# Row one-hots of eight tokens as one VectorE comparison, and the low parts of 64 table blocks on GpSimd

## The chip, the cores and the metric

The kernel runs on one core of a Trainium2 chip. The metric is the device time of one execution in microseconds (us). Three runs of the kernel before took 2293.08, 2294.5 and 2297.16 us; their median, 2294.5 us, is the time to compare with.

## The reference, cut to what matters

The reference is one layer of a hybrid network over 128 prompt tokens and 512 sample tokens of width 1024. Its last part is a mixer of 16384 experts, and the change touches only that part:

```python
q = (x @ wq).reshape(T, 8, 2, 128)                    # 8 heads, two half queries
s = einsum('thpd,hpkd->thpk', q, sub_keys)            # scores against 2 x 128 keys
s_top, i_top = top_k(s, 16)                           # pairs of keys -> best 16 experts
idx  = i_top[..., 0, a] * 128 + i_top[..., 1, b]      # expert = 128 * i + j
gate = softmax(best)
a = gelu(einsum('td,tkd->tk', x, u_tab[idx]))         # 128 chosen experts a token
y = einsum('tk,tkd->td', gate * a, v_tab[idx])
```

## The kernel before, in words

For the 512 sample tokens the kernel does not gather rows. It multiplies the whole table `u` with the tokens: 128 blocks of 128 experts, `ps = u_block x h2` (K = 1024 in 8 steps `k` of 128, N = 512 tokens), takes the gelu and stores the result (`a_dram`). To keep the accuracy of float32, each operand is split in a high part (a cast to fp32r) and a low part (the rest), and each step `k` has three matmuls: `uhi*h2hi`, `uhi*h2lo`, `ulo*h2hi` (L906). A block of `u` is loaded by SP (`load_u`, L516, 512 KB), ScalarE casts it (`uhi`, L1682), and another engine subtracts (`ulo = uraw - uhi`). In blocks 0 to 40 that engine is GpSimd (L1812), from block 41 on it is VectorE (L1417). `uhi` and `ulo` have two buffers each, `uraw` four.

In blocks 40 to 103, the gate stage, the dense gate matrix of each of the 512 sample tokens is built besides, eight tokens a block. For one token the 128 chosen experts stand on the partitions with their numbers i and j and their gate. `eA[:, q]` (128x128) has the gate where the column equals i, else 0, and `eB[:, k]` has 1 where the column equals j: each is a comparison of `iota` with one column of `cols_hk`. The matmul `eB x eA` (L946) gives the 128x128 gates of the token. It stands behind step `k` of the block's products (`gate_matrix(k)`), so that in each block eight steps of three products and one gate matrix follow each other on TensorE. `eA` is a ring of 8 matrices, `eB` two groups of eight. Four tokens fill a PSUM bank; ScalarE copies it to `gst` (L1708), and when eight blocks are done SP stores the half in two DMAs of 2 MB (`store_g`, L543), the first behind the block whose number is 7 modulo 8, the second behind the next. Before each of them SP has stored the block's gelu output (`store_a`, L521) and loaded block n+4.

Who makes what in the gate stage before the change:

- VectorE, per block (`step_b`): eight `eA` (L1452), the two `eB` with q % 4 == 3 (L1451), behind the fifth token `split_u` of block n+1 (L1417), and two `dot` (L1426). A dot is a product-sum of 1024 elements of one gathered row for each of the 128 prompt tokens, `ugat` with `h2row`. Its loop over four groups of 16 blocks is one body run without a loop and then a hardware loop of three passes; a pass begins with copies of the group's columns to `jcur` and `cur`, since an address that depends on the loop counter is only used there.
- GpSimd, per block: the other six `eB` (L1855), and two `gather_u` (L1824), indirect DMAs of 128 rows of 4 KB, 512 KB each, into a ring of four slots. The gathers behind the six `eB` of block m (counted from the first gate block) are those for the dots of block m+1. A gather waits until the dot that used its slot is done.
- ScalarE, per block: `split_u(n+1)` (`uhi`), two copies to `gst`, and the gelu (L1692), in this order.
- SP, per block: `store_a(n)`, `load_u(n+4)`, and where due `store_g`.

TensorE waits at the start of a block for `uhi` and `ulo` of the block, and before a gate matrix for its `eA` and `eB`. VectorE may write `eA` of token q when the gate matrix of token q-8 is done. The order on each engine is the order of the program; nothing reorders it.

Of the kernel before, what the change touches and what calls it, by code (L numbers as in the profile page):

```python
# [8 lines left out]
ALU = mybir.AluOpType  # L9
# [8 lines left out]
P = 128  # L18
# [54 lines left out]
POOL_ROWS = TB - TB // 4  # L73

CAND = [(0, 2, 16), (2, 2, 8), (4, 4, 4), (8, 8, 2)]
NCAND = sum(na * nb for _, na, nb in CAND)


def dve_row(q):
    return q % 4 == 3  # L80
# [14 lines left out]
def bass_hybrid_layer(nc, x, cvec, w_ada, w_in, w_out, w_q, cols, hfcols, hf_w1, hf_w2, hf_w3,  # L95
# [7 lines left out]
    with ctx:  # L103
# [71 lines left out]
        cur = at("cur", 134, [P, 3, 128])  # L175
        jcur = at("jcur", 136, [P, 128])
# [222 lines left out]
        cur_ready = sem("cur_ready")  # L399
# [21 lines left out]
        jcur_ready = sem("jcur_ready")  # L421
# [185 lines left out]
        def _(pe):  # L607
# [324 lines left out]
            def step_b(it, first):  # L932
                for b in range(NB_B):

                    def gate_matrix(k):
# [7 lines left out]
                        if not dve_row(q):  # L943
                            pe.wait_ge(onehot_j_ready, (it * NB_B + b) * POOL_ROWS + k - k // 4 + 1)
# [47 lines left out]
        def _(dve):  # L992
# [426 lines left out]
            def dot(it, k, first):  # L1419

                if k == 0 and not first:
                    dve.wait_ge(dots_gelu, it)
                if not (first and k == 0):
                    dve.wait_ge(dot_done, it * DOTS_IT + k)
                dve.wait_ge(u_gathered[k % GSLOT], it * (16 * DOTS_IT // GSLOT) + 16 * (k // GSLOT + 1))
                dve.tensor_tensor_reduce(junk[:], ugat[:, k % GSLOT], h2row[:], 1.0, 0.0, ALU.mult, ALU.add,  # L1426
                                         dots[:, k:k + 1]).then_inc(dot_done, 1)

            def slot_weights(it):

                hk = bass.ds(it * DOTS_IT, DOTS_IT)
                dve.wait_ge(dots_gelu, it + 1)
                dve.tensor_tensor(w0[:, hk], acur[:], gate0[:, hk], ALU.mult).then_inc(w0_ready, 1)

            def step_b(it, first):
                if not first:
                    dve.wait_ge(onehot_j_ready, it * POOL_ROWS * NB_B)
                    dve.wait_ge(onehot_ready, it * P)
                dd = bass.ds(it * P, P)
                dve.tensor_copy(jcur[:], cols_hk[:, 1, dd]).then_inc(jcur_ready, 1)  # L1440
                dve.tensor_copy(cur[:], cols_hk[:, :, dd]).then_inc(cur_ready, 1)
                dve.wait_ge(cur_ready, it + 1)
                for b in range(NB_B):
                    n = it * NB_B + b + BLK_A
                    for k in range(TB):
                        q = TB * b + k
                        tok = it * P + q
                        if not (first and q < RING):
                            dve.wait_ge(onehot_used, tok + 1 - RING)
# [6 lines left out]
                    if b == 2 and not first:  # L1456
                        slot_weights(it - 1)
                    for e in range(DOTS_B):
                        dot(it, DOTS_B * b + e, first)

            loop(dve, NTD, step_b)
# [321 lines left out]
        def _(pool):  # L1783
# [161 lines left out]
```

## Time and profile before

| | |
|---|---|
| median of three runs | 2294.5 us |
| the profiled execution: its own time / span | 2292.26 / 2290.5 us |
| TensorE matmul busy, share of the span | 2173.6 us, 95% |
| VectorE busy | 1438.7 us, 63% |
| ScalarE busy | 623.6 us, 27% |
| GpSimd busy | 796.5 us, 35% |
| mean granted TensorE clock | 0.976 |
| moved by DMA | 475.54 MB, 208 GB/s over the span |

Matmuls overlap, so a busy TensorE is not one at its peak. The gate stage lasts from 917.8 to 1442 us of the span. The stages behind it are the other 24 blocks of `u` and the second products with the table `v`.

### The profile page before, as it was taken

The page shows a single profiled execution, that of the slowest core. Times are in us where ns is not written, and L with a number is a line of the kernel's source. Part 1 is how long each engine was busy: PE and PEld are TensorE (multiplying, and loading weights), DVE is VectorE, ACT ScalarE, POOL GpSimd, SP SyncE. Part 2 cuts the span into 40 slices and gives each one's busy share as a digit, 9 for nine tenths or more (in the row PEclk, how much of TensorE's full clock was granted, in tenths as well). Part 3 has the DMA queues.
Part 4 walks back from the last instruction along what each step waited for, and adds up shares of the span by engine and source line. Part 5 has one row for each costly group of instructions (what it writes and reads, how often), then busy time and mean ns, then how long its engine had stood idle before and what let it go on. Part 6 is the DMA issues. An engine that isn't in the chain of part 4 may idle for free.

```text
span 2290.5 us, 30680 instructions
## 1 busy us (share of the span) xinstructions
PE 2173.6 (95%) x9868; PEld 1665.6 (73%) x9868; DVE 1438.7 (63%) x3055; ACT 623.6 (27%) x930; POOL 796.5 (35%) x713
## 2 busy tenths in 40 slices
PE   7999998798989999999999898999999999999998
PEld 3554444546987877877777787787888888888886
DVE  4221426334889998878777787324766666666665
ACT  2111012333222223333333233223323222222222
POOL 0000001003225554998989898001222212121220
PEclk7999999898999999999999999999999999999999
DMA  9122124204204444699997899855988888888883
GB/s 338 45 74 72 44 85 181 97 33 160 75 1 153 144 139 138 205 301 309 297 282 250 270 298 288 254 174 210 352 285 294 285 291 289 289 288 290 288 289 146
DMA packets 293477, 475.54 MB, mean 208 GB/s; under 512 B 148871, under 2 KB 150055, under 8 KB 292872
## 3 DMA queue, kind: packets, MB, share of 16 engines
q1 hardware_dynamic: 256520, 340.20, 45.1%
q0 software_dynamic: 36864, 134.23, 16.6%
q8 instruction: 42, 0.69, 0.1%
q14 instruction: 51, 0.42, 0.1%
HBM read 401.76 MB, written 72.61 MB: 207 GB/s over the span
## 4 chain that ended last, share of the span: by engine, by line
PE 78%; POOL 9%; DVE 5%; DMA 3%; issue 2%; SPq 2%; ACT 1%; DVEq 0%; ACTq 0%; POOLq 0%
PE ps L965 30%; PE ps L906 19%; POOL eB L1855 6%; PE ps L624 5%; PE ps L717 3%; PE ps L843 3%; POOL ugat L1824 3%; PE ps L878 3%; PE ps L879 3%; PE ps L683 2%; PE ps L946 2%; SPq L521 2%; PE ps L623 1%; DMA uraw<-in_u_t 1%; PE ps L666 1%
## 5 line engine op out<-in xcount | busy, mean ns | idle before, releaser
L906 PE MATMUL ps<-h2hi,uhi 128*128 128x512 f32 x1024 | 449.8, 439 | 20.3 <-DVE scores L1375 7.7
L906 PE MATMUL ps<-h2hi,ulo 128*128 128x512 f32 x1024 | 404.9, 395 | 0.0
L965 PE MATMUL ps<-vhi,whi 128*128 128x512 f32 x1024 | 399.2, 390 | 5.6 <-DVE wlo L1475 5.6
L906 PE MATMUL ps<-h2lo,uhi 128*128 128x512 f32 x1024 | 403.7, 394 | 0.0
L965 PE MATMUL ps<-vhi,wlo 128*128 128x512 f32 x1024 | 399.1, 390 | 0.0
L965 PE MATMUL ps<-vlo,whi 128*128 128x512 f32 x1024 | 399.0, 390 | 0.0
L1832 POOL DMA_INDIRECT vgat<-in_v_tab,idx x128 | 145.4, 1136 | 660.0 <-DVE y L1485 508.3
L1855 POOL TENSOR_SCALAR eB<-iota,jcur 128x128 f32<-128x128 f32 x384 | 318.1, 841 | 18.8 <-DVE jcur L1440 17.0
L1473 DVE TENSOR_TENSOR vlo<-vraw,vhi 128x1024 fp32r<-128x1024 f32 x128 | 156.8, 1225 | 216.6 <-ACT vhi L1748 216.6
L1748 ACT ACTIVATE vhi<-vraw 128x1024 fp32r<-128x1024 f32 x128 | 135.5, 1061 | 465.8 <-PE ps L965 464.0
L946 PEld LDWEIGHTS ps<-eA,eB 128*128 128x128 f32 x1024 | 192.2, 191 | 93.0 <-POOL eB L1855 25.6
L946 PE MATMUL ps<-eA,eB 128*128 128x128 f32 x1024 | 202.4, 279 | 35.4 <-DVE eA L1452 24.6
L906 PEld LDWEIGHTS ps<-h2hi,uhi 128*128 128x128 f32 x1024 | 196.8, 192 | 44.5 <-issue 21.1
L965 PEld LDWEIGHTS ps<-vhi,whi 128*128 128x128 f32 x1024 | 192.6, 188 | 46.8 <-issue 6.8
L906 PEld LDWEIGHTS ps<-h2hi,ulo 128*128 128x128 f32 x1024 | 194.7, 190 | 43.0
L1417 DVE TENSOR_TENSOR ulo<-uraw,uhi 128x1024 fp32r<-128x1024 f32 x87 | 109.5, 1258 | 182.9 <-ACT uhi L1682 180.5
L965 PEld LDWEIGHTS ps<-vlo,whi 128*128 128x128 f32 x1024 | 192.6, 188 | 40.1
L965 PEld LDWEIGHTS ps<-vhi,wlo 128*128 128x128 f32 x1024 | 192.5, 188 | 40.1
L906 PEld LDWEIGHTS ps<-h2lo,uhi 128*128 128x128 f32 x1024 | 197.0, 192 | 19.9
L1426 DVE CUSTOM_DVE_ANT_0 junk<-ugat,h2row 128x1024 f32<-128x1024 f32 x128 | 157.5, 1230 | 24.6 <-DMA ugat<-in_u_rows,idx 21.8
L1452 DVE TENSOR_SCALAR eA<-iota,cur 128x128 f32<-128x128 f32 x512 | 168.2, 372 | 0.4
L1708 ACT ACTIVATE gst<-ps 128x512 f32<-128x512 f32 x128 | 76.5, 598 | 329.5 <-PE ps L946 329.5
(270 smaller groups left out, 2993.7 us busy)
## 6 DMA issues: line engine op xcount, KB each, us to landing
uraw<-in_u_t SPq DMA_DIRECT2D x128, 512.0 KB
vraw<-in_v_tab SPq DMA_DIRECT2D x128, 512.0 KB
gelu_scratch<-aout SPq DMA_DIRECT2D x128, 256.0 KB
gate_scratch<-gst SPq DMA_DIRECT2D x16, 2048.0 KB, 14.9
ain<-gelu_scratch SPq DMA_DIRECT2D x128, 256.0 KB, 4.1
gin<-gate_scratch SPq DMA_DIRECT2D x128, 256.0 KB, 4.4
wring<-in_w_ada SPq DMA_DIRECT2D x12, 2048.0 KB, 10.6
wring<-in_w_in SPq DMA_DIRECT2D x6, 2048.0 KB, 8.5
```

The source lines that it names most:

```text
L624: s_ = pe.matmul(bank(us)[0:m], w, as_, start=(j == 0), stop=(j == n - 1))
L906: last = pe.matmul(ps[:, b % 4, :], w[:, b % 2, k, :], h[:, k, LP:T], start=(k == 0 and j == 0), stop=(k == KD - 1 and j == 2))
L946: pe.matmul(o_, eB[:, b % 2, k], eA[:, q % RING], start=True, stop=True).then_inc(onehot_used, 1)
L965: last = pe.matmul(ps[:, y_bank(t) + h, :], w[:, b, (t - 1) * P:t * P], v[:, b, h * 512:(h + 1) * 512], start=(start and j == 0), stop=(st ...
L1417: dve.tensor_tensor(ulo[:, b % 2], uraw[:, b % 4], uhi[:, b % 2].bitcast(F32), ALU.subtract).then_inc(ulo_ready, 1)
L1426: dve.tensor_tensor_reduce(junk[:], ugat[:, k % GSLOT], h2row[:], 1.0, 0.0, ALU.mult, ALU.add, dots[:, k:k + 1]).then_inc(dot_done, 1)
L1452: dve.tensor_scalar(eA[:, q % RING], iota[:], cur[:, 0, q:q + 1], cur[:, 2, q:q + 1], ALU.is_equal, ALU.mult).then_inc(onehot_ready, 1)
L1473: dve.tensor_tensor(vlo[:, s], vraw[:, s], vhi[:, s].bitcast(F32), ALU.subtract).then_inc(vlo_ready, 1)
L1708: act.activation(gst[:, half, :, off:off + 4], ps[:, 4 + quad % 4, :].rearrange("p (q i) -> p i q", q=4), ACT.Copy).then_inc(gate_staged, 1)
L1748: act.activation(vhi[:, s], vraw[:, s], ACT.Copy).then_inc(vhi_ready, 1)
L1832: pool.indirect_dma_start(out=vgat[:, k % GSLOT], out_offset=None, in_=v_tab, in_offset=bass.IndirectOffsetOnAxis(ap=idx0[:, k:k + 1], axis=0)
L1855: pool.tensor_scalar(eB[:, b % 2, k], iota[:], jcur[:, TB * b + k:TB * b + k + 1], None, ALU.is_equal).then_inc(onehot_j_ready, 1)
```

## The change

Three things change, all in the gate stage:

1. `eB` of all eight tokens of a block is one VectorE instruction (`slot_keys`), a `tensor_tensor` comparison of 128x1024 elements whose two inputs are broadcast views of `iota` and of eight columns of `cols_hk`. It is written one block ahead. GpSimd writes no `eB`. TensorE waits for it once a block.
2. The low parts `ulo` of blocks 41 to 104 are made by GpSimd, in front of the two gathers of its step; VectorE takes over again from block 105.
3. VectorE's loop over groups is written out (64 blocks one after another), without `cur` and `jcur`; the columns are read from `cols_hk`.

```diff
-                        if not dve_row(q):
-                            pe.wait_ge(onehot_j_ready, (it * NB_B + b) * POOL_ROWS + k - k // 4 + 1)
+                        if k == 0:
+                            pe.wait_ge(onehot_j_ready, it * NB_B + b + 1)
...
-            def step_b(it, first):
-                if not first:
-                    dve.wait_ge(onehot_j_ready, it * POOL_ROWS * NB_B)
-                    dve.wait_ge(onehot_ready, it * P)
-                dd = bass.ds(it * P, P)
-                dve.tensor_copy(jcur[:], cols_hk[:, 1, dd]).then_inc(jcur_ready, 1)
-                dve.tensor_copy(cur[:], cols_hk[:, :, dd]).then_inc(cur_ready, 1)
-                dve.wait_ge(cur_ready, it + 1)
-                for b in range(NB_B):
...
-                        if dve_row(q):
-                            dve.tensor_scalar(eB[:, b % 2, k], iota[:], cur[:, 1, q:q + 1], None, ALU.is_equal)
-                        dve.tensor_scalar(eA[:, q % RING], iota[:], cur[:, 0, q:q + 1], cur[:, 2, q:q + 1],
-                                          ALU.is_equal, ALU.mult).then_inc(onehot_ready, 1)
-                        if k == 4:
-                            split_u(n + 1, b + 1)
...
-            loop(dve, NTD, step_b)
+            def slot_keys(m):
+                if m >= 2:
+                    dve.wait_ge(onehot_used, TB * (m - 1))
+                dve.tensor_tensor(eB[:, m % 2], iota[:].unsqueeze(1).broadcast_to([P, TB, 128]),
+                                  cols_hk[:, 1, TB * m:TB * (m + 1)].unsqueeze(2).broadcast_to([P, TB, 128]),
+                                  ALU.is_equal).then_inc(onehot_j_ready, 1)
+            slot_keys(0)
+            for n in range(BLK_A, BLK_C):
+                m = n - BLK_A
+                for k in range(TB):
+                    q = TB * m + k
+                    if q >= RING:
+                        dve.wait_ge(onehot_used, q + 1 - RING)
+                    dve.tensor_scalar(eA[:, q % RING], iota[:], cols_hk[:, 0, q:q + 1], cols_hk[:, 2, q:q + 1],
+                                      ALU.is_equal, ALU.mult).then_inc(onehot_ready, 1)
+                if m % NB_B == 2 and m >= NB_B:
+                    slot_weights(m // NB_B - 1)
+                if n + 1 < BLK_C:
+                    slot_keys(m + 1)
+                for e in range(DOTS_B):
+                    dot(DOTS_B * m + e)
+            dve.wait_ge(ulo_ready, BLK_C + 1)
...
             for n in range(NTD * NB_B):
-                it, b = n // NB_B, n % NB_B
-                if b == 0:
-                    pool.wait_ge(jcur_ready, it + 1)
-                if n >= 2:
-                    pool.wait_ge(onehot_used, TB * (n - 1))
-                for k in range(TB):
-                    if not dve_row(TB * b + k):
-                        pool.tensor_scalar(eB[:, b % 2, k], iota[:], jcur[:, TB * b + k:TB * b + k + 1], None, ALU.is_equal
-                                           ).then_inc(onehot_j_ready, 1)
+                split_u(BLK_A + n + 1, n + 1, False)
                 if n:
                     for e in range(DOTS_B):
                         gather_u(DOTS_B * (n - 1) + e + GSLOT)
```

## Rows read from the trace of the kernel before

**Rows 1.** Busy time in a window, the gate stage (columns in the first line).

```profile
core 0: us, PE busy (x) PEld busy (x) DVE busy (x) ACT busy (x) POOL busy (x), PEclk, DMA share, GB/s
917.80:1442.00 524.20, 488.83 (x2571) 408.44 (x2570) 410.61 (x971) 168.26 (x259) 466.64 (x508) 0.98 0.89 277
```

**Rows 2.** Timeline of ScalarE (start, length): gelu of four blocks; 919.92 and 1442.48 are 64 blocks apart.

```profile
919.92 0.60 ACT L1692 ACTIVATE aout<-ps 128x512 f32<-128x512 f32 x1 [8.58 <-PE ps L906]
971.75 0.59 ACT L1692 ACTIVATE aout<-ps 128x512 f32<-128x512 f32 x1
...
979.08 0.59 ACT L1692 ACTIVATE aout<-ps 128x512 f32<-128x512 f32 x1
979.56 1.06 ACT L1682 ACTIVATE uhi<-uraw 128x1024 fp32r<-128x1024 f32 x1
...
1442.48 0.59 ACT L1692 ACTIVATE aout<-ps 128x512 f32<-128x512 f32 x1
```

**Rows 3.** Timeline of GpSimd, one block of a stretch without gate stores.

```profile
1206.86 5.47 POOL L1855 TENSOR_SCALAR eB<-iota,jcur 128x128 f32<-128x128 f32 x6
1212.50 1.91 POOL L1824 DMA_INDIRECT ugat<-in_u_rows,idx  x1 [0.17 <-issue]
1214.71 0.94 POOL L1824 DMA_INDIRECT ugat<-in_u_rows,idx  x1 [0.30 <-issue]
1215.68 5.24 POOL L1855 TENSOR_SCALAR eB<-iota,jcur 128x128 f32<-128x128 f32 x6
```

**Rows 4.** Timeline of VectorE and TensorE, start of VectorE's third and fourth passes.

```profile
1173.02 0.23 DVE L1440 COPY jcur<-cols_hk 128x128 f32 x1 [3.34 <-issue]
1174.32 0.71 PE L946 MATMUL ps<-eA,eB 128*128 128x128 f32 x2 [3.36 <-DVE eA L1452]
1311.83 0.23 DVE L1440 COPY jcur<-cols_hk 128x128 f32 x1 [2.79 <-issue]
```

**Rows 5.** Timeline of SP's queue, around the first pair of gate stores, and the last.

```profile
980.64 2.11 SPq L543 DMA_DIRECT2D gate_scratch<-gst  x1
987.03 6.35 SPq L521 DMA_DIRECT2D gelu_scratch<-aout  x1
993.90 0.49 SPq L543 DMA_DIRECT2D gate_scratch<-gst  x1
994.44 13.03 SPq L521 DMA_DIRECT2D gelu_scratch<-aout  x1
1242.93 0.38 SPq L543 DMA_DIRECT2D gate_scratch<-gst  x1
1376.22 0.38 SPq L543 DMA_DIRECT2D gate_scratch<-gst  x1
1444.42 9.01 SPq L543 DMA_DIRECT2D gate_scratch<-gst  x2
```

**Rows 6.** Chain of waits, the three late table blocks (start, length).

```profile
1007.56 7.05 DMA uraw<-in_u_t
1272.35 8.75 DMA uraw<-in_u_t
1403.42 9.27 DMA uraw<-in_u_t
```

**Rows 7.** Timeline of ScalarE, VectorE and TensorE at the first late block.

```profile
1014.64 1.06 ACT L1682 ACTIVATE uhi<-uraw 128x1024 fp32r<-128x1024 f32 x1 [4.64 <-DMA uraw<-in_u_t]
1015.73 1.42 DVE L1417 TENSOR_TENSOR ulo<-uraw,uhi 128x1024 fp32r<-128x1024 f32 x1 [5.30 <-ACT uhi L1682]
1017.51 0.80 PE L946 MATMUL ps<-eA,eB 128*128 128x128 f32 x2 [3.36 <-DVE eA L1452]
1019.39 0.63 PE L946 MATMUL ps<-eA,eB 128*128 128x128 f32 x2
1020.98 0.39 PE L946 MATMUL ps<-eA,eB 128*128 128x128 f32 x2
```

**Rows 8.** Timeline, blocks 0 to 40: GpSimd's subtraction alone, and beside VectorE.

```profile
705.51 2.45 POOL L1812 TENSOR_TENSOR ulo<-uraw,uhi 128x1024 fp32r<-128x1024 f32 x1 [3.05 <-ACT uhi L1682]
710.95 4.47 POOL L1812 TENSOR_TENSOR ulo<-uraw,uhi 128x1024 fp32r<-128x1024 f32 x1 [2.99 <-ACT uhi L1682]
710.88 2.29 DVE L1364 TENSOR_TENSOR oneh<-work,iota 128x2048 f32<-128x2048 f32 x1
713.21 4.35 DVE L1367 TENSOR_TENSOR oneh<-oneh,itopf 128x2048 f32<-128x2048 f32 x1
```

**Rows 9.** Timeline of VectorE: second dots of three blocks that waited for their rows.

```profile
1082.29 1.23 DVE L1426 CUSTOM_DVE_ANT_0 junk<-ugat,h2row 128x1024 f32<-128x1024 f32 x1 [0.65 <-DMA ugat<-in_u_rows,idx]
1138.04 1.23 DVE L1426 CUSTOM_DVE_ANT_0 junk<-ugat,h2row 128x1024 f32<-128x1024 f32 x1 [0.78 <-DMA ugat<-in_u_rows,idx]
1246.66 1.23 DVE L1426 CUSTOM_DVE_ANT_0 junk<-ugat,h2row 128x1024 f32<-128x1024 f32 x1 [0.55 <-DMA ugat<-in_u_rows,idx]
```

**Rows 10.** Timeline of GpSimd: the gathers of those rows, in the same order.

```profile
1073.95 0.94 POOL L1824 DMA_INDIRECT ugat<-in_u_rows,idx  x1 [0.30 <-issue]
1129.25 0.94 POOL L1824 DMA_INDIRECT ugat<-in_u_rows,idx  x1 [0.30 <-issue]
1240.37 0.94 POOL L1824 DMA_INDIRECT ugat<-in_u_rows,idx  x1 [0.30 <-issue]
```

More of the change, by code:

```diff
@@ L174, in bass_hybrid_layer @@
         eB = at("eB", 126, [P, 2, TB, 128])
-        cur = at("cur", 134, [P, 3, 128])
-        jcur = at("jcur", 136, [P, 128])
         gst = at("gst", 139, [P, 2, 128, 64])
@@ L398, in bass_hybrid_layer @@
         dot_done = sem("dot_done")
-        cur_ready = sem("cur_ready")
         dots_gelu = sem("dots_gelu")
@@ L420, in bass_hybrid_layer @@
         onehot_used = sem("onehot_used")
-        jcur_ready = sem("jcur_ready")
         gate_full = sem("gate_full")
@@ L1417, in split_u, with dot @@
                 dve.tensor_tensor(ulo[:, b % 2], uraw[:, b % 4], uhi[:, b % 2].bitcast(F32), ALU.subtract).then_inc(ulo_ready, 1)
[L1419 to L1426, printed above, removed]
+            def dot(g):
+                r, k = g // DOTS_IT, g % DOTS_IT
+                if k == 0 and r:
+                    dve.wait_ge(dots_gelu, r)
+                if g:
+                    dve.wait_ge(dot_done, g)
+                dve.wait_ge(u_gathered[g % GSLOT], 16 * (g // GSLOT + 1))
+                dve.tensor_tensor_reduce(junk[:], ugat[:, g % GSLOT], h2row[:], 1.0, 0.0, ALU.mult, ALU.add,
@@ L1427, in dot, with slot_weights @@
                                          dots[:, k:k + 1]).then_inc(dot_done, 1)
-            def slot_weights(it):
-                hk = bass.ds(it * DOTS_IT, DOTS_IT)
-                dve.wait_ge(dots_gelu, it + 1)
+            def slot_weights(r):
+                hk = slice(r * DOTS_IT, (r + 1) * DOTS_IT)
+                dve.wait_ge(dots_gelu, r + 1)
                 dve.tensor_tensor(w0[:, hk], acur[:], gate0[:, hk], ALU.mult).then_inc(w0_ready, 1)
-            def step_b(it, first):
-                if not first:
-                    dve.wait_ge(onehot_j_ready, it * POOL_ROWS * NB_B)
-                    dve.wait_ge(onehot_ready, it * P)
-                dd = bass.ds(it * P, P)
-                dve.tensor_copy(jcur[:], cols_hk[:, 1, dd]).then_inc(jcur_ready, 1)
-                dve.tensor_copy(cur[:], cols_hk[:, :, dd]).then_inc(cur_ready, 1)
-                dve.wait_ge(cur_ready, it + 1)
-                for b in range(NB_B):
-                    n = it * NB_B + b + BLK_A
-                    for k in range(TB):
[L1446 to L1449, printed above, removed]
-                        if dve_row(q):
-                            dve.tensor_scalar(eB[:, b % 2, k], iota[:], cur[:, 1, q:q + 1], None, ALU.is_equal)
-                        dve.tensor_scalar(eA[:, q % RING], iota[:], cur[:, 0, q:q + 1], cur[:, 2, q:q + 1],
-                                          ALU.is_equal, ALU.mult).then_inc(onehot_ready, 1)
-                        if k == 4:
-                            split_u(n + 1, b + 1)
[L1456 to L1459, printed above, removed]
@@ L1847, in _ @@
             for n in range(NTD * NB_B):
-                it, b = n // NB_B, n % NB_B
-                if b == 0:
-                    pool.wait_ge(jcur_ready, it + 1)
-                if n >= 2:
-                    pool.wait_ge(onehot_used, TB * (n - 1))
-                for k in range(TB):
-                    if not dve_row(TB * b + k):
-                        pool.tensor_scalar(eB[:, b % 2, k], iota[:], jcur[:, TB * b + k:TB * b + k + 1], None, ALU.is_equal
-                                           ).then_inc(onehot_j_ready, 1)
+                split_u(BLK_A + n + 1, n + 1, False)
                 if n:
```

3 lines of the change are left out of this document (removed).

## The prediction

> **What bounds the kernel now.** I read the page first (TensorE is busy nearly all the time, so only a stage in which it idles can change), then the windows of the gate stage, ScalarE's timeline as a clock of the blocks, the waits, and the timelines of each engine where a block was long. In the window of the gate stage TensorE is busy 488.8 of 524.2 us, GpSimd 466.6, and the DMA engines 0.89 of the time at 277 GB/s [rows 1]. So three things are close to full at once, and the question is which of them ends each block.
>
> The starts of ScalarE's gelu tell the pace. An undisturbed block takes 979.08 - 971.75 = 7.33 us, all of it TensorE. The 64 blocks take 1442.48 - 919.92 = 522.6 us against 64 x 7.33 = 469.1 [rows 2]. The excess, 53.5 us, is all that the change can win in this stage, and it has three sources:
> - *GpSimd's own pace.* In a stretch without gate stores one round of six `eB` and two gathers lasts 1215.68 - 1206.86 = 8.8 us [rows 3]. That is 1.5 more than a block of TensorE; between 1204 and 1242 us there are five such blocks, and elsewhere the same work mostly takes less than 7.33: about 8 us in all.
> - *VectorE's loop passes.* At the third and fourth pass VectorE starts nothing for 3.34 and 2.79 us and TensorE's next gate matrix comes 3.36 us late [rows 4]. With the slow clock behind it (below) the two blocks are 4.6 and 5.2 us long: 10 us. TensorE and ScalarE cross their own loop ends there without a gap of their own.
> - *Gate stores.* Behind each 2 MB store SP's next issue is held: 6.35 us, then 13.03 [rows 5]. So the table block five blocks on is asked for 27 us after the first store (1007.56 - 980.64) and lands 7.05 to 9.27 us later [rows 5, 6]. That is the rest, 53.5 - 8 - 10 = 35 us over seven pairs of stores.
>
> **Part 1, the end of GpSimd's `eB` and of the loop.** Six `eB` of about 0.9 us (5.47 / 6) [rows 3] leave GpSimd; the 8 us of slow rounds go. The written-out loop has no pass ends: 10 us go, but both lie in or near a pair of stores, and what the stores cost does not vanish with them. The Trainium skill says on "Runtime: NRT & Kernel Launch" (Instruction fetch mechanics) that a taken branch out of the prefetched window stalls until the page is fetched; rows 4 agree, and by that rule alone the 10 us would be won in full.
>
> **Part 2, one comparison on VectorE.** The same kind of instruction (two broadcast views, `is_equal`) takes 2.29 us for 2048 elements [rows 8], so 1.15 for 1024. VectorE loses `ulo` (about 1.23) and two small `eB`. It has 8 `eA`, 1.15 and two dots of 1.23 in 7.33 us, some 5.8: no bound. It runs nearly a block ahead of TensorE, so this is hidden. What is gained: before, `split_u` stood in the middle of VectorE's row. When a table block was late, VectorE waited in it 5.30 us and the sixth gate matrix of the block *before* the late one came 3.36 us late [rows 7]. After, this block runs to its end.
>
> **Part 3, `ulo` on GpSimd.** Alone it takes 2.45 us [rows 8]; `uhi` starts 0.48 behind the gelu and takes 1.06 [rows 2]. It needs to be there when the next block starts and is, by over 2 us. The subtraction itself is hidden. But two gathers are queued behind it. Count from the first gate matrix of block m, at 0 (the gelu of the block before starts then too). `uhi` of block m+1 ends at 1.54, `ulo` at 4.0, the gathers are issued at 4.15 and, with the spacing of rows 3 when nothing holds the first, 5.5. Their rows are for the dots of block m+1, and behind these dots stand the `eA` of block m+2. From issue to use a gather needs L; then a dot (1.23) and an `eA` (0.35). So the first gate matrix of block m+2, due at 14.67, is free at 5.5 + L + 1.6 = 7.1 + L. TensorE keeps its pace if L is below 7.6. L read from dots that waited: 6.29 us in a stretch without stores (1246.66 - 1240.37), 8.34 and 8.79 beside them (1082.29 - 1073.95, 1138.04 - 1129.25) [rows 9, 10]. Quiet blocks pass; beside stores two blocks cost 7.1 + 8.6 - 14.67 = 1.0 us more, hidden behind the late table block.
>
> **A pair of stores after the change.** Time from the first store, t = 0. The late block lands at 34.0, 38.2 or 36.5 (1007.56 + 7.05 - 980.64, 1272.35 + 8.75 - 1242.93, 1403.42 + 9.27 - 1376.22) [rows 5, 6], mean 36.2. Then `uhi` 1.06, `ulo` 2.45 and the handoffs, 0.4: TensorE starts the block at 40.1. At its own pace it would have been there at 34.4 (five blocks from 979.08, less the 0.7 of the first products, less 980.64). Stall: 5.7 us. After a stall TensorE runs at the lower of its two levels for a while: the gate matrices of rows 7 are 1.88 and 1.59 us apart, against 0.92. That adds 1.7. Third, the gathers for this block's dots were behind the late `ulo`: issued 0.1 and 1.45 behind the start of the block. With L = 8.3 the next block's first gate matrix is free 1.45 + 8.3 + 1.6 = 11.35 behind it; TensorE would want it at 8.0 + 1.7 = 9.7. That adds 1.65. Before, the gathers went out during the stall and were never late behind it. Sum: 5.7 + 1.7 + 1.65 = 9.05 us a pair, 7 pairs in the stage: 63.4 us.
>
> **The sum.** Excess before 53.5, after 63.4: +9.9 us on the profiled execution's 2292.26, so 2302. Its time lies 2.2 us below the median of the runs shown, inside their spread of 4; I leave that. The costs not seen before: L in a block just behind a stall, from 6.3 to 8.8, is -1.65 to +0.5 a pair, -12 to +4; the landing from 34.0 to 38.2 is -2.2 to +2.0 a pair, -15 to +14. VectorE's new wait for `eB`'s buffer is met before it is reached.
>
> **The port.** A subtraction of GpSimd that met a two-input VectorE instruction took 4.47 instead of 2.45, and the VectorE instruction behind it 4.35 instead of 2.29 [rows 8]: each waited for the other's end. In the gate stage the two-input instructions are short (1.15 to 1.23), so `ulo` can come up to 1.2 later. The Trainium skill ("SBUF — State Buffer", on VectorE and GpSimd contention) calls this an exclusive lock held for the whole instruction, taken with two SBUF inputs; by it, `eB` on VectorE would hold GpSimd's subtraction in every block, which is the third rival.
>
> **The rivals.**
> - *The gathers are in time (faster).* If L behind a stall is about 6.3, the third term is 0; and with every landing as the first (34.0) the stall is 3.5. Then 3.5 + 1.7 = 5.2 a pair, 36 in all, 17 less than before: 2275; with the landings half way, 2285. For it: the 6.29 of the quiet stretch, and VectorE no longer coupled to the table's load. Against: three table loads and three gelu stores are issued at once just when the gathers go. It decides at L = 6.7.
> - *The stores set the pace of the half-group.* If TensorE, early or late, meets the same store end, won and lost cancel: 2290 to 2297. For it: the half-groups of before are 66.3 us on average ((1444.42 - 980.64) / 7) [rows 5], with and without a loop end in them.
> - *The port decides.* With `ulo` held 1.2 in every block the bound is 8.3 + L for two blocks; at L = 7.3 that is 0.45 a block more, for the 29 blocks away from stores 13, and 1.2 for each pair: +21 on the forecast, 2323, less where VectorE's dots have moved away: 2315 to 2323. Against it: when the dots come later, they leave the time of `ulo` free.
>
> **How the numbers follow.** A difference under 0.2% (4.6 us) can't be told from none. The forecast, slower (2298 to 2309), has 0.38, the port 0.10, the stores' pace 0.16, the gathers in time 0.36. That gives slower 0.48, same 0.16, faster 0.36. The likeliest is 2302. The range reaches over the gathers' case to 2277 and into the port's to 2318.
>
> **What would show it.** After the change: GpSimd's rounds well under 7.33 us with waits for `uhi` in front of `ulo`; no gap in VectorE at the pass ends; undisturbed blocks at 7.33; at a late table block, TensorE waiting for `ulo` at the start of the block instead of at the sixth gate matrix; behind it dots waiting for their gather and TensorE for `eA`. I am wrong if these dots don't wait (then it is faster), if `ulo` takes over 3 us in most blocks, or if the late table block lands at another time than 34 to 38 us behind the first store.

## The result, and the profile after

The changed kernel took 2318.95 us (median of 8 runs, 2304.12 to 2338.19), the kernel before 2293.79 us in the same session (8 runs). The ratio is 1.0113, with a 95% interval of 1.008 to 1.0145: slower, as forecast, but by 25 us instead of 10, and 1 us outside the range. The profiled execution took 2312.91 us, 20.65 more than that of before.

The starts of the gelu on ScalarE's timeline again give the pace (start, length). 919.86 and 1460.92 are 64 blocks apart, the middle two are neighbours:

```profile
919.86 0.60 ACT L1681 ACTIVATE aout<-ps 128x512 f32<-128x512 f32 x1 [8.56 <-PE ps L896]
...
1166.21 0.59 ACT L1681 ACTIVATE aout<-ps 128x512 f32<-128x512 f32 x1
1174.11 0.59 ACT L1681 ACTIVATE aout<-ps 128x512 f32<-128x512 f32 x1
...
1460.92 0.59 ACT L1681 ACTIVATE aout<-ps 128x512 f32<-128x512 f32 x1
```

The stage takes 1460.92 - 919.86 = 541.1 us against 522.6 [rows 2]; so 18.5 of the 20.65 us are lost in it. Over 64 blocks of 7.33 us the excess is 72.0 us (53.5 before). I split it by the length of the blocks, taken from all 64 gelu starts: 

| excess over 7.33 us a block | before | forecast after | after |
|---|---|---|---|
| blocks over 9 us | 33.1 (6 blocks) | 63.4 (7 pairs of stores) | 48.4 (10 blocks) |
| all other blocks | 20.4 (58) | 0 | 23.6 (54) |
| sum | 53.5 | 63.4 | 72.0 |

The blocks up to 9 us have 20.4 us of excess before the change too; what the change adds to them in this split is small, and experiments 7 to 9 and 12 separate it better.

Two windows of the changed kernel, columns as in [rows 1]: the window of [rows 1], which now ends 19 us before the stage does, and one stretch of it:

```profile
917.80:1442.00 524.20, 479.79 (x2470) 397.16 (x2469) 458.09 (x807) 162.17 (x249) 350.93 (x182) 0.96 0.87 268
1098.00:1222.00 124.00, 117.63 (x619) 95.94 (x618) 117.28 (x202) 41.00 (x64) 92.46 (x48) 1.00 0.93 289
```

GpSimd's busy time fell from 466.6 to 350.9 us, but VectorE's rose from 410.6 to 458.1, although it has fewer instructions (807 records against 971). In the second window it is busy 117.28 of 124 us. Where that comes from is in the page's groups (busy, mean ns of one | idle before it, and its releaser):

```profile
L1801 POOL TENSOR_TENSOR ulo<-uraw,uhi 128x1024 fp32r<-128x1024 f32 x105 | 285.8, 2723 | 279.4 <-ACT uhi L1671 279.3
L1417 DVE CUSTOM_DVE_ANT_0 junk<-ugat,h2row 128x1024 f32<-128x1024 f32 x128 | 186.2, 1455 | 64.5 <-DMA ugat<-in_u_rows,idx 62.7
L1442 DVE TENSOR_SCALAR eA<-iota,cols_hk 128x128 f32<-128x128 f32 x512 | 222.1, 508 | 9.1 <-PE ps L936 9.1
L1813 POOL DMA_INDIRECT ugat<-in_u_rows,idx x128 | 198.8, 1553 | 30.7 <-issue 23.2
```

The mean `eA` took 372 ns before and takes 508, the mean dot 1230 and now 1455, the mean issue of a gather 1191 and now 1553. The dots and the gathers are as before; `eA` now reads its columns from `cols_hk`, and in experiment 5, which changes that alone, it takes 376 ns. One quiet block of the timeline of VectorE, GpSimd and TensorE shows how it happens:

```profile
1166.22 4.35 DVE L1442 TENSOR_SCALAR eA<-iota,cols_hk 128x128 f32<-128x128 f32 x8
1167.82 2.40 POOL L1801 TENSOR_TENSOR ulo<-uraw,uhi 128x1024 fp32r<-128x1024 f32 x1 [0.72 <-ACT uhi L1671]
1170.37 3.29 POOL L1813 DMA_INDIRECT ugat<-in_u_rows,idx  x1 [0.15 <-issue]
1170.48 1.21 DVE L1430 TENSOR_TENSOR eB<-iota,cols_hk 128x1024 f32<-128x1024 f32 x1
1171.62 1.21 DVE L1417 CUSTOM_DVE_ANT_0 junk<-ugat,h2row 128x1024 f32<-128x1024 f32 x1
...
1172.87 1.22 DVE L1417 CUSTOM_DVE_ANT_0 junk<-ugat,h2row 128x1024 f32<-128x1024 f32 x1
1173.96 0.94 POOL L1813 DMA_INDIRECT ugat<-in_u_rows,idx  x1 [0.30 <-issue]
1174.02 4.22 DVE L1442 TENSOR_SCALAR eA<-iota,cols_hk 128x128 f32<-128x128 f32 x8
1174.49 0.48 PE L936 MATMUL ps<-eA,eB 128*128 128x128 f32 x2 [0.22 <-DVE eA L1442]
```

Eight `eA` take 4.35 us here when the subtraction falls among them; in the stage, 19 groups of eight that run without a gap and that no subtraction touches take 2.18 us on average, 38 groups that one falls into 4.32. I call this lengthening the hold. The first gather is issued for 3.29 us instead of 0.94, beside `eB` and the dots. The block is 7.90 us long and TensorE waits for its first `eA`. The next two views show what this does to a late row gather. First the tile `eA` between 944 and 949 us (shortest/median/longest in ns), then the timeline around it:

```profile
L1442 DVE TENSOR_SCALAR eA<-iota,cols_hk x8: 333/334/2353, 944.6 to 948.4; 128x128 f32<-128x128 f32 x8
```

```profile
943.45 1.23 DVE L1417 CUSTOM_DVE_ANT_0 junk<-ugat,h2row 128x1024 f32<-128x1024 f32 x1 [2.61 <-DMA ugat<-in_u_rows,idx]
943.96 2.92 POOL L1801 TENSOR_TENSOR ulo<-uraw,uhi 128x1024 fp32r<-128x1024 f32 x1 [1.06 <-ACT uhi L1671]
947.06 0.76 PE L936 MATMUL ps<-eA,eB 128*128 128x128 f32 x2 [4.55 <-issue]
...
986.36 1.90 POOL L1813 DMA_INDIRECT ugat<-in_u_rows,idx  x1 [0.30 <-issue]
997.13 2.34 POOL L1801 TENSOR_TENSOR ulo<-uraw,uhi 128x1024 fp32r<-128x1024 f32 x1 [2.25 <-ACT uhi L1671]
997.26 3.29 DVE L1417 CUSTOM_DVE_ANT_0 junk<-ugat,h2row 128x1024 f32<-128x1024 f32 x1 [3.19 <-DMA ugat<-in_u_rows,idx]
1000.48 2.22 DVE L1442 TENSOR_SCALAR eA<-iota,cols_hk 128x128 f32<-128x128 f32 x8
1000.92 0.77 PE L936 MATMUL ps<-eA,eB 128*128 128x128 f32 x2 [5.23 <-issue]
```

One of the eight `eA` takes 2353 ns instead of 334 (the longest in the stage, at 1102.93, takes 3147): it ends with the subtraction at 946.9, and TensorE starts at 947.06. The profile calls the 4.55 us "issue", but what ended them is that `eA`. At 997.26 the dot, already late for its rows, is held to the subtraction's end at 999.47 and so takes 3.29 us; TensorE is idle 5.23 us. With the lower clock behind it (three products in 1.28 us instead of 0.70 in the chain of waits) each such stall costs about 7 us (behind 947.06 the granted clock is 0.61 on average over 7 us). The table block itself is late for TensorE in two places only:

```profile
1228.55 1.06 ACT L1671 ACTIVATE uhi<-uraw 128x1024 fp32r<-128x1024 f32 x1 [6.70 <-DMA uraw<-in_u_t]
1229.69 2.35 POOL L1801 TENSOR_TENSOR ulo<-uraw,uhi 128x1024 fp32r<-128x1024 f32 x1 [8.93 <-ACT uhi L1671]
1232.14 0.49 PE L896 MATMUL ps<-h2hi,uhi 128*128 128x512 f32 x1 [3.73 <-ACT uhi L1671]
...
1369.30 0.76 PE L896 MATMUL ps<-h2hi,uhi 128*128 128x512 f32 x1 [3.17 <-ACT uhi L1671]
```

TensorE waits for `uhi` and `ulo` together, and the profile names `uhi`. But `uhi` ends at 1229.61 (1366.46 in the second place) and `ulo` at 1232.04 (1369.20), 0.1 us before TensorE starts: both waits end with the subtraction.

### The profile page after: what moved, and what is told of

Its sections match the earlier page's. It is cut to its first block, busy times and chain, and to the rows that moved or that the text cites. A ratio compares the mean times of both kernels' runs of the same rounds, so it can differ in the third digit from the quotient of the medians.

```text
span 2311.1 us, 29384 instructions
## 1 busy us (share of the span) xinstructions
PE 2185.2 (95%) x9868; PEld 1671.8 (72%) x9868; DVE 1499.9 (65%) x2919; ACT 623.4 (27%) x930; POOL 697.3 (30%) x393
## 3 DMA queue, kind: packets, MB, share of 16 engines
q0 software_dynamic: 36864, 134.23, 16.6%
## 4 chain that ended last, share of the span: by engine, by line
PE 78%; DVE 7%; DMA 5%; SPq 3%; issue 3%; POOL 2%; ACT 2%; ACTq 0%; DVEq 0%; POOLq 0%
PE ps L955 30%; PE ps L896 19%; PE ps L614 5%; DMA ugat<-in_u_rows,idx 3%; PE ps L707 3%; PE ps L833 3%; SPq L511 3%; PE ps L868 3%; PE ps L869 2%; PE ps L936 2%; PE ps L673 2%; PE ps L613 1%; POOL ulo L1801 1%; DVE eA L1442 1%; DMA uraw<-in_u_t 1%
## 5 line engine op out<-in xcount | busy, mean ns | idle before, releaser
L1801 POOL TENSOR_TENSOR ulo<-uraw,uhi 128x1024 fp32r<-128x1024 f32 x105 | 285.8, 2723 | 279.4 <-ACT uhi L1671 279.3
L1417 DVE CUSTOM_DVE_ANT_0 junk<-ugat,h2row 128x1024 f32<-128x1024 f32 x128 | 186.2, 1455 | 64.5 <-DMA ugat<-in_u_rows,idx 62.7
L1442 DVE TENSOR_SCALAR eA<-iota,cols_hk 128x128 f32<-128x128 f32 x512 | 222.1, 508 | 9.1 <-PE ps L936 9.1
L1813 POOL DMA_INDIRECT ugat<-in_u_rows,idx x128 | 198.8, 1553 | 30.7 <-issue 23.2
```

The costliest lines, as they stand in the source:

```text
L1417: dve.tensor_tensor_reduce(junk[:], ugat[:, g % GSLOT], h2row[:], 1.0, 0.0, ALU.mult, ALU.add, dots[:, k:k + 1]).then_inc(dot_done, 1)
L1442: dve.tensor_scalar(eA[:, q % RING], iota[:], cols_hk[:, 0, q:q + 1], cols_hk[:, 2, q:q + 1], ALU.is_equal, ALU.mult).then_inc(onehot_read ...
L1801: pool.tensor_tensor(ulo[:, b % 2], uraw[:, b % 4], uhi[:, b % 2].bitcast(F32), ALU.subtract).then_inc(ulo_ready, 1)
L1813: pool.indirect_dma_start(out=ugat[:, k % GSLOT], out_offset=None, in_=u_rows, in_offset=bass.IndirectOffsetOnAxis(ap=idx0[:, k:k + 1], ax ...
```

## The experiments

Times are medians, ratios are to the kernel before on the same chip. The stage is the 64 blocks between the two gelu starts. "Changed" is the kernel after the change.

**1. Gathers ahead of the low part** (changed kernel).

```diff
-                split_u(BLK_A + n + 1, n + 1, False)
                 if n:
                     for e in range(DOTS_B):
                         gather_u(DOTS_B * (n - 1) + e + GSLOT)
+                split_u(BLK_A + n + 1, n + 1, False)
```

> The changed kernel (2319 us) with one edit: in each round of GpSimd in the gate stage the two gathers are issued before the low part, not behind it; the low part may then start later, nothing else moves. Order theory (the gathered rows come late because their issue waits for uhi and ulo; behind the late dots stands eA, and TensorE waits for it): the issue moves some 5 us forward, the dots hardly wait for a gather, undisturbed blocks go from 7.8 back to 7.33 us, and the stall behind a late table block is single; 2280 to 2300 us. Port theory (GpSimd's subtraction of 2.4 us holds VectorE's eA, dots and eB, wherever the gathers stand): the subtraction is as long and as frequent, so 2312 to 2325 us.

2305.71 us, ratio 1.0062 (1.0034 to 1.0091). No dot waits for its gather, no block is over 9 us, and yet the stage takes 527.2 us, since nearly every block takes 8.40. Its window, and its timeline:

```profile
1098.00:1222.00 124.00, 112.98 (x596) 92.61 (x596) 123.52 (x195) 39.22 (x61) 79.16 (x45) 1.00 0.89 282
```

```profile
1215.12 4.94 DVE L1442 TENSOR_SCALAR eA<-iota,cols_hk 128x128 f32<-128x128 f32 x8
1217.32 2.40 POOL L1801 TENSOR_TENSOR ulo<-uraw,uhi 128x1024 fp32r<-128x1024 f32 x1
...
1223.52 4.95 DVE L1442 TENSOR_SCALAR eA<-iota,cols_hk 128x128 f32<-128x128 f32 x8
```

VectorE is busy 123.52 of 124 us: its row is 4.94 of `eA`, then `eB` and two dots, 8.40 in all, as each of them starts just before the one ahead of it has ended. The `eA` lose 2.76 us to a subtraction of 2.40: the one that is held starts 0.66 us before the subtraction's recorded start, in most blocks, and ends 0.09 behind its end. The median lies between the two expectations, but the trace settles the mechanism. The late gathers are one loss (they go with the order), the hold another, and without the first the second alone sets the block. The stage is 4.6 us longer than that of before, the profiled execution 14.3; the rest lies in front of the stage and behind it (see what stays open, below).

**2. A second subtraction on GpSimd** (added to experiment 1).

```diff
+                pool.tensor_tensor(spare[:], h2row[:], h2row[:], ALU.subtract).then_inc(spare_done, 1)
```

> The kernel with the gathers first (2306 us, blocks of 8.40 us, VectorE without a gap) with a second subtraction of 1024 elements on GpSimd in each round, behind the low part; its output is used by nobody. GpSimd's own work is then 2.4 + 2.4 + 2.8 us a round, under 8.4. Port theory (VectorE runs no instruction of this stage while GpSimd subtracts, so the block is VectorE's own 5.9 us plus GpSimd's 2.4): the block grows by 2.4 to 10.8 us, 64 times: 2440 to 2465 us. If the 8.40 us come from anything else (late rows, stores, the length of the program): 2300 to 2320 us.

2374.89 us, ratio 1.0344 (1.0283 to 1.0406), two runs; blocks of 9.23 us.

```profile
1209.43 3.94 POOL L1804 TENSOR_TENSOR ulo<-uraw,uhi 128x1024 fp32r<-128x1024 f32 x1
...
1211.16 3.29 DVE L1420 CUSTOM_DVE_ANT_0 junk<-ugat,h2row 128x1024 f32<-128x1024 f32 x1
1213.33 2.87 POOL L1847 TENSOR_TENSOR spare<-h2row 128x1024 f32<-128x1024 f32 x1
1214.38 3.69 DVE L1445 TENSOR_SCALAR eA<-iota,cols_hk 128x128 f32<-128x128 f32 x8
```

More of GpSimd's work lengthens VectorE's row, which nothing in the program connects with it: the dot is held 2.06 us and the `eA` 1.5. That is the hold. The time lies between the two expectations. The price was 0.83 us a block instead of the 2.4 expected, because the `eA` are held less (3.69 instead of 4.94) and GpSimd waits too (3.94 for `ulo`).

**3. The low parts back on VectorE, gathers alone on GpSimd** (changed kernel).

```diff
                                       ALU.is_equal, ALU.mult).then_inc(onehot_ready, 1)
+                    if k == 4:
+                        split_u(n + 1, n + 1)
...
-                split_u(BLK_A + n + 1, n + 1, False)
```

> The changed kernel with the low parts back on VectorE (behind the fifth eA, as before the change); GpSimd then only issues gathers. eB stays one VectorE comparison and the loop stays written out. Order theory and port theory both: the loss is gone, GpSimd has no round of its own and the loop ends are gone, so as before or faster, 2275 to 2294 us. A theory that VectorE itself has become too full (eB of 1.2 us in front of the dots delays them and the eA behind them): stays slow, 2310 or more, since VectorE has 1.2 us more in each block than in the changed kernel.

2320.83 us, ratio 1.0109 (1.0073 to 1.0144). This missed: the mean `eA` is back at 351 ns, but seven blocks of 15.3 to 17.6 us stand behind the seven pairs of stores, 59.1 us of excess in these seven. The table block comes later. The last pair on SP's queue (first gate store; second gate store; the store of the gelu output, held; the table load behind it):

```profile
1408.08 0.38 SPq L533 DMA_DIRECT2D gate_scratch<-gst  x1
...
1425.54 0.44 SPq L533 DMA_DIRECT2D gate_scratch<-gst  x1
1426.16 12.77 SPq L511 DMA_DIRECT2D gelu_scratch<-aout  x1
1439.18 0.35 SPq L506 DMA_DIRECT2D uraw<-in_u_t  x1
```

The table load goes out 31.1 us behind the first store (27.2 before: 1403.42 - 1376.22, [rows 5, 6]). Without `eB` GpSimd has its gathers out as soon as a slot is free; I took it that they fill the DMA queues ahead of the stores, and tried that next.

**4. The same, with the gathers held back** to where TensorE has done the fourth gate matrix.

```diff
+                    pool.wait_ge(onehot_used, TB * n + 4)
                     for e in range(DOTS_B):
                         gather_u(DOTS_B * (n - 1) + e + GSLOT)
```

> The version with the low parts back on VectorE and only gathers on GpSimd (2320.8 us, blocks up to 17.6 us behind each pair of stores), with one wait more on GpSimd: the gathers of block m are issued only when TensorE has done the fourth gate matrix of the block, so at about the place in the block where the kernel before issues them behind its six eB. What is computed is the same. Theory 'the row gathers' place': the gathers that run ahead pile up in front of the stores and the table block (late table block at +31 us of the first store, +27 before), so with this wait the late table block is at +27 again, the pair costs some 5 us less and the time is 2285 to 2300. Rival 'the half-group's pace is the stores alone': the table block stays at +31, and the time is 2312 to 2325.

2288.97 us, ratio 0.9997 (0.9971 to 1.0024). One wait more, and 0.8 us below the kernel before in that session where experiment 3 was 28.7 above it. The stage takes 513.5 us. The last pair:

```profile
1383.83 0.38 SPq L533 DMA_DIRECT2D gate_scratch<-gst  x1
...
1398.35 0.38 SPq L533 DMA_DIRECT2D gate_scratch<-gst  x1
1398.91 10.62 SPq L511 DMA_DIRECT2D gelu_scratch<-aout  x1
1409.79 0.35 SPq L506 DMA_DIRECT2D uraw<-in_u_t  x1
```

The table load goes out 26.0 us behind the first store, and the blocks over 9 us have 26.6 us of excess instead of 59.1. So the place of the gathers decides what a pair of stores costs. This kernel has all of the change but the low parts on GpSimd, and a wait besides, and takes as long as the kernel before. Against the changed kernel it is 26 us faster (each against the kernel before of its session), and its stage is 28 us shorter. That the low parts on GpSimd cost this much holds with this wait; without it (experiment 3) taking them away wins nothing, because the gathers move too. With the stores spread the same edit needs no such wait (experiments 7 and 9). Of the rest of the change the times show no gain; in the trace the stage is 9 us shorter than before, and the 12 us by which it starts later take that back.

**5. The kernel before with VectorE's loop written out,** nothing else (`step_b` as 64 blocks, columns read from `cols_hk`).

> The kernel before (2294 us) with VectorE's loop over the four groups written out and the columns read from cols_hk, without cur and jcur; eB and ulo stay where they were. By the prediction's first part the two gaps at the loop ends (3.3 and 2.8 us, with the slow clock 10 us) go: 2284 to 2291 us. If the gate stores set the pace of each half-group anyway: 2291 to 2295. If the written-out program itself costs something: above 2298.

2292.16 us, ratio 0.9986 (0.9962 to 1.0009). No difference clear of noise. The gaps at the pass ends are gone, and the stage takes 525.7 us: seven blocks of 11.2 to 18.9 us behind the stores take back what was won.

**6. The low part in two halves of 512 elements** (changed kernel).

```diff
+                    for g in range(2):
+                        kk = slice(4 * g, 4 * g + 4)
+                        last = pool.tensor_tensor(ulo[:, b % 2, kk], uraw[:, b % 4, kk], uhi[:, b % 2, kk].bitcast(F32),
+                                                  ALU.subtract)
```

> The changed kernel with GpSimd's low part as two instructions of 512 elements instead of one of 1024. Order theory: the gathers come as late as before or 0.1 us later, so no gain: 2317 to 2326 us. Port theory: a VectorE instruction that meets the subtraction waits for 1.2 us at most instead of 2.4, so 5 to 15 us faster: 2304 to 2314 us.

2328.0 us, ratio 1.0154 (1.0122 to 1.0187), above both expectations. The two halves take 1737 ns each on average (median 1.33 us, mean 1.74), together nearly a third more than the whole in the stage (2.64); GpSimd is done later, and dots wait 93 us for gathers instead of 63. Shorter instructions don't help here: each of them can be held anew. It tells the theories apart no further.

**7. to 9. The gate stores spread.** Each half is stored in eight transfers of 512 KB, one a block, in place of two of 2 MB; in the changed kernel, in the kernel before, and in the version of experiment 3.

```diff
-                ii = slice(64 * part_, 64 * part_ + 64)
+                ii = slice(16 * part_, 16 * part_ + 16)
...
-                    if b == 0 and not first:
-                        store_g(it * 2 - 1, 1, 1)
-                    elif b == HALF:
-                        store_g(it * 2, 0, 1)
+                    elif b < HALF:
+                        if not first:
+                            store_g(it * 2 - 1, 1, b + 1)
+                    else:
+                        store_g(it * 2, 0, b - HALF + 1)
```

> The changed kernel (2319 us) with each half of the gate matrix stored in eight DMAs of 512 KB, one behind each block, instead of two of 2 MB; the same bytes and the same 256-byte rows. Stores theory (SP is held behind the 2 MB stores, the table block five on lands late, and the gathers behind its low part are late too, 9 us a pair): these stalls go, the 7.8 us of the quiet blocks by the port stay: stage about 500 instead of 541 us, 2272 to 2285 us. If the whole loss of the change is the port and the order, and the stores only fill time that is lost anyway: 2305 to 2320 us.

> The kernel before (2294 us) with the same eight small stores a half. Stores theory: of its 53 us over 64 blocks of 7.33 the 35 us behind stores go, GpSimd's own pace and the loop ends stay: 2255 to 2268 us. If the DMA engines are simply full in this stage (they need 322 GB/s at full pace): 2275 to 2294 us.

> The kernel with eB and the low parts on VectorE (2321 us, seven stalls of 8 us behind the stores and blocks of 7.33 to 7.6 else) with the eight small stores. Stores theory: its loss against the kernel before is only that its faster blocks and its earlier gathers meet the same stores; without the 2 MB stores it is the fastest of all, stage 475 to 485 instead of 543 us: 2252 to 2265 us. If VectorE is too full with eB and low part: 2290 or more, and slower than the kernel before with small stores.

| | us | ratio | stage, us | median block | blocks over 9 us |
|---|---|---|---|---|---|
| changed kernel | 2299.22 | 1.0013 (0.9988 to 1.0039) | 516.1 | 7.79 | 3 |
| kernel before | 2264.43 | 0.9877 (0.9837 to 0.9916) | 486.4 | 7.33 | 2 |
| low parts on VectorE | 2259.47 | 0.9841 (0.9798 to 0.9883) | 478.1 | 7.48 | 0 |

Without the bursts the changed kernel is 40 us slower than the same kernel with the low parts on VectorE, and its stage 38 us longer. This is the plainest price of the low parts on GpSimd, in one session and by one edit. Of the excess over 7.33 us a block, the blocks up to 9 us have 30.4 in the one and 9.0 in the other, the blocks over 9 us 16.6 and 0. For the kernel before, the stage is 36 us shorter with the stores spread: the 35 us that the prediction put down to them. The group of `eA` in the one and in the other:

```profile
L1444 DVE TENSOR_SCALAR eA<-iota,cols_hk 128x128 f32<-128x128 f32 x512 | 253.0, 570 | 2.7 <-PE ps L938 2.7
```

```profile
L1444 DVE TENSOR_SCALAR eA<-iota,cols_hk 128x128 f32<-128x128 f32 x512 | 142.4, 351 | 0.0
```

So the hold costs without stores as well. The two long blocks left in the kernel before (11.7 and 13.6 us) are VectorE's pass ends, which now show on their own:

```profile
1168.10 0.23 DVE L1442 COPY jcur<-cols_hk 128x128 f32 x1 [2.75 <-issue]
1291.98 0.23 DVE L1442 COPY jcur<-cols_hk 128x128 f32 x1 [4.67 <-issue]
```

**10. Experiment 1 with the stores spread.**

> The version with the two gathers in front of the low part on GpSimd (2305.7 us, every block 8.40 us, VectorE without a gap), with each gate half stored in eight transfers of 512 KB, one a block, in place of two of 2 MB. Port theory: the 8.40 us are VectorE's own row of work, lengthened because its instructions and GpSimd's subtraction hold each other; with the stores spread the blocks stay at 8.3 to 8.5 and the time at 2298 to 2310, although the same change of the stores gave 20 us on the changed kernel and 29 on the kernel before. Rival, 'DMA traffic sets the 8.40': blocks drop to 7.4 to 7.8 and the time to 2260 to 2285.

2307.39 us, ratio 1.0064 (1.0041 to 1.0087): no different from experiment 1. The blocks stay at 8.40 us. Where VectorE's row is the bound, the stores cost nothing and spreading them brings nothing.

**11. The kernel before, written out and with the stores spread.**

> The kernel before with VectorE's loop over groups written out (alone: no gain, ratio 0.9986) and the gate halves stored in eight transfers of 512 KB, one a block. With the stores spread the kernel before took 2264.4 us, and its two blocks over 9 us (11.7 and 13.6) were the two pass ends. Theory: the pass ends cost about 10 us and the pairs of stores hid that; here it shows: 2250 to 2258, no block over 9 us. Rival: the pass ends cost nothing even so: 2260 to 2268.

2250.75 us, ratio 0.9817 (0.9774 to 0.9859). No block is over 9 us, the stage takes 478.8. Beside experiment 8 the intervals of the ratios overlap; the two long blocks are gone in the trace. This is the fastest version by its median, 39 us below the 2289.78 us of the kernel before in that session and some 64 below the changed one, which was 25 above the kernel before in its own; experiment 9 (0.9841, 0.9798 to 0.9883) can't be told from it.

**12. One input in place of two for GpSimd's instruction** (experiment 7).

```diff
+                pool.tensor_scalar(ulo[:, b % 2], uraw[:, b % 4], 0.5, None, ALU.mult).then_inc(ulo_ready, 1)
```

> The changed kernel with the gate halves stored in eight transfers of 512 KB (2299.2 us), and with GpSimd's instruction for blocks 41 to 104 reading one input in place of two: uraw times 0.5, same size and output, same waits, same place in GpSimd's order. The low parts are then not the reference's. Port theory: what costs is that a two-input instruction of GpSimd and VectorE's instructions hold each other. With one input the eight eA of a block take some 2.3 to 2.8 us again (4.2 before), gathers are no longer held to 3.3 us, the quiet blocks are 7.33 to 7.5, and the time is within 15 us of the version with the low parts on VectorE (2259.5): 2252 to 2275. Rival 1, 'GpSimd's row': that the gathers stand behind an instruction of 2.4 us that waits for uhi is what costs: the eA are short but dots wait for gathers, 2285 to 2302. Rival 2: one-input instructions hold VectorE as well: eA stay at 4.2 and the time at 2295 to 2305.

2279.37 us, ratio 0.9932 (0.9904 to 0.9959): between the port theory (to 2275) and the first rival (from 2285). The output of this kernel is not the reference's, since the low parts are wrong.

A block in which the instruction falls fully beside the `eA`, and one in which it does not:

```profile
1111.37 3.50 DVE L1444 TENSOR_SCALAR eA<-iota,cols_hk 128x128 f32<-128x128 f32 x8
1111.42 2.77 POOL L1812 TENSOR_SCALAR ulo<-uraw 128x1024 fp32r<-128x1024 f32 x1 [1.98 <-ACT uhi L1673]
...
1165.20 2.14 DVE L1444 TENSOR_SCALAR eA<-iota,cols_hk 128x128 f32<-128x128 f32 x8
1167.25 1.22 DVE L1432 TENSOR_TENSOR eB<-iota,cols_hk 128x1024 f32<-128x1024 f32 x1
1167.77 3.33 POOL L1812 TENSOR_SCALAR ulo<-uraw 128x1024 fp32r<-128x1024 f32 x1 [1.69 <-ACT uhi L1673]
1170.22 1.23 DVE L1419 CUSTOM_DVE_ANT_0 junk<-ugat,h2row 128x1024 f32<-128x1024 f32 x1 [1.74 <-DMA ugat<-in_u_rows,idx]
1171.27 1.04 POOL L1820 DMA_INDIRECT ugat<-in_u_rows,idx  x1 [0.17 <-issue]
```

One input holds the `eA` too, but less: 3.4 to 3.5 us for eight in the five blocks with 2.7 us or more of overlap, against 4.31 with 2.4 us of overlap in experiment 7. There are also fewer overlaps (36 of 64 groups have none, 8 of 64 in experiment 7), since VectorE's row has become shorter and runs ahead. The second rival is out: eight `eA` don't take 4.2 us any more.

By the times some 18 of the 40 us are back, but not in the way that this suggests. The stage takes 509.1 us, only 7.0 less than in experiment 7 and 31 more than in experiment 9; the other 11 us by which the two profiled executions differ lie outside it. Inside it, two things cancel:

| excess over 7.33 us a block | experiment 7, two inputs | experiment 12, one input | experiment 9, on VectorE |
|---|---|---|---|
| blocks up to 9 us | 30.4 | 9.1 | 9.0 |
| blocks over 9 us | 16.6 (3) | 30.9 (7) | 0 |

The quiet blocks are as good as with the low parts on VectorE (median 7.33 us), so the 21 us that they had lost go with the two-input hold. The long blocks grow: dots wait 106 us (23 in experiment 7) for gathers that stand behind an instruction which is longer (median 2.79 us) than the two-input one (2.40). So the port theory holds for the quiet blocks and the first rival for the long ones. How large the rival's share is with an instruction of 2.40 us can't be read from this, since the instruction tried is itself longer.

## Why the prediction was right or wrong

*Right: the sign, and that the low part on GpSimd is what speaks against the change.* Experiments 7 and 9 show its price, and experiment 4 that the rest of the change leaves the time where it was.

*The step that failed: "VectorE ... some 5.8: no bound" and, from it, "Quiet blocks pass".* The 5.8 us were durations of VectorE's instructions without a GpSimd subtraction beside them, while the step moves one into every block. Beside it a block's row is up to 2.8 us longer (4.94 for `eA` instead of 2.14), 8.40 in experiment 1. I had the row that showed it, the 4.35 of [rows 8], and used it only in the other direction: as a delay of `ulo`, and only for VectorE's instructions that read two tensors. I did not ask what happens to the `eA`, which stand exactly where `uhi` is done. The term was 0, and blocks up to 9 us had 23.6 us of excess. Not all of that is the hold: versions with neither hold nor bursts keep 9.0 and 9.7 us there (experiments 9 and 11), which the forecast had also put at nothing. With the stores spread the hold alone makes it 30.4 instead of 9.0.

The Trainium skill ("SBUF — State Buffer", SBUF: two separate sides) says that the one that starts first has the shared ports for its whole instruction. The runs agree where the dot at 997.26 waits for the end at 999.47. They don't in two places: in experiment 1 the held `eA` starts, as recorded, 0.66 us ahead of the subtraction, and in experiment 12 a GpSimd instruction of 2.77 us among eight `eA` makes 2.18 us of them into 3.50, so that some of them run while it does. By the page VectorE's instructions take part if they have two inputs in SBUF or run in a two-port mode. Which of the two the `eA` fall under, with one tensor and two columns as operands, no run shows; that they are held, one of them for 3147 ns in all, the trace does, and so they have to be counted.

*"A pair of stores after the change", 9.05 us, 63.4 in all: too large, and made of other parts.* Its first term, 5.7 for a table block whose `ulo` is late, had the right mechanism in two pairs, where it was 3.73 and 3.17, and was nothing in five. The load itself was much as forecast: in the four pairs where ScalarE waited for it, `uhi` started 32.1, 35.2, 37.0 and 38.1 us behind the first store. What must differ is where TensorE stood by then; that it had been delayed elsewhere and was not early any more fits the long blocks in front, but was not measured pair by pair. The third term, 1.65 for late dots, was the large one: idle times of 4.0 to 5.2 us in four places, with about 7 us each. There L was outside its bounds of 6.3 to 8.8: the gather of 986.36 was used at 997.26, L = 10.9, and over the 44 dots that waited it was 5.1 to 10.9 (24 dots before, 6.1 to 9.6). The hold stands in this chain at the dot. At the issue it may add too: the five gathers whose issue took over 3 us and whose dot waited were used 9.2 to 9.8 us after it began. But issues of 1.8 us in experiments 1 and 9 landed no later after their start than those of 1.0 (7.4 and 7.4 us; 6.8 and 7.4), so this part is not shown. Blocks over 9 us had 48.4 us of excess.

*"The written-out loop ... 10 us go": right in the trace, worthless by itself* (experiment 5). The remark that the stores' cost does not vanish with it was the right one; the gain shows only when the stores are spread, and there in the trace alone (the two blocks of 11.7 and 13.6 us; the stage 486.4 and then 478.8).

*"`eB` 1.15":* 1.21. *"The subtraction itself is hidden":* right in the quiet blocks; behind the late load TensorE waits for it, as the first term of a pair had it.

*The rivals.* "The port decides" (0.10; 2315 to 2323) came nearest and has the time, but that is partly luck. It is the port, yet not as this rival had it: there VectorE holds `ulo` for 1.2 us in every block, and measured, `ulo` takes 2.41 us in the median and over 3 in 8 of 64 blocks. The hold went the other way, onto the `eA`, and its price is in VectorE's row, not in L. "The stores set the pace" (0.16) describes experiment 5, not the change. "The gathers are in time" (0.36) had far too much: experiment 1 has them in time, and is slower than before.

*What stays open.* How the cost of the low part divides between the hold and the gathers' delay is known only roughly, 21 to 17 us by the length of the blocks with the stores spread (experiments 7 and 9), and with the bursts not at all. Outside the stage the profiled executions differ by up to 16 us (1768 to 1784), in places that no edit touches: six of the fourteen, those of experiments 1 to 4, 7 and 9, have a block near 740 us of the span that takes 14.5 to 15.3 us, where the others take 9.0, and start the stage later. Why is not known, and a difference of times under some 10 us between two versions can't be put down to the stage by itself. That earlier gathers lengthen SP's hold is shown; by which queue they do it is not.

## What to carry to other kernels

Before work is moved between VectorE and GpSimd, sum up each engine's row with the durations that its instructions have beside the other engine's two-input instructions, not alone; look for a row in the trace where the two overlap, and use it in both directions. Where transfers are close to full (0.89 here), a burst of large stores can decide what everything else is worth: spread it first, since then gains that were swallowed appear. Compare the stage in the traces beside the times, and split its excess into many short losses and few long ones, since an edit can move the two in opposite directions. And an engine that is freed issues its transfers earlier, which can cost more than the engine's time was worth.

## What the runs showed of the hardware

- Beside a GpSimd subtraction of 1024 elements (2.40 us) single 128-element VectorE comparisons took up to 3147 ns (334 alone) and 1024-element dots 3.29 us (1.23). The comparison that is held can start, as recorded, 0.66 us before the subtraction does.
- Beside `eB` and two dots the issue of an indirect DMA on GpSimd took 3.29 us (0.94 alone), over 3 us 12 times in the stage. Whether the rows land later by it is not shown.
- Beside a one-input GpSimd instruction of the same size eight `eA` took 3.5 us, beside the two-input one 4.3, alone 2.2; the one-input instruction itself took 2.79 us, the two-input one 2.40.
- Eight stores of 512 KB, one a block, in place of two of 2 MB in neighbouring blocks, with the same bytes, were worth 30 us for the kernel before (ratio 0.9877), and nothing where VectorE's row was the bound (experiments 1 and 10).
